# First block's gates and branch products with the tokens on the partitions, and their sum turned for the mixing projection

## The chip, the cores and the metric

The kernel runs on one core of a Trainium2 chip. The metric is the device time of one execution in microseconds (us). TensorE is called PE below, its weight load PEld, VectorE DVE, ScalarE ACT, GpSimd POOL and SyncE SP.

## The reference

Two transformer blocks, one after the other, on 256 tokens of width 1024, in fp32. The change touches the end of the first block's mixer:

```python
h = rms_norm(x, mix_norm_g[l])
(c_b, c_c, c_u, f_q, f_k, f_v, f_g, s_q, s_k, s_v, gate_logits) = split_proj(h @ w_in[l])
y_conv = short_conv_branch(c_b, c_c, c_u, conv_w[l])
y_fox = fox_branch(f_q, f_k, f_v, f_g, forget_bias[l])
y_swa = swa_sink_branch(s_q, s_k, s_v, rel_bias, sink[l])
gates = jax.nn.sigmoid(gate_logits.reshape(b, s, N_BRANCH, D_MODEL))
merged = (gates[:, :, 0] * (y_conv @ w_branch[l, 0])
          + gates[:, :, 1] * (y_fox @ w_branch[l, 1])
          + gates[:, :, 2] * (y_swa @ w_branch[l, 2]))
x = x + merged @ w_mix_out[l]
x = x + cross_attention(rms_norm(x, xattn_norm_g[l]), ...)
```

The gate logits are a 1024 x 3072 projection, each branch product is 512 x 1024, and the mixing projection is 1024 x 1024. After this come cross attention, a SwiGLU feed-forward, and the whole second block (a bidirectional recurrent mixer, spatial gating, another feed-forward).

## The kernel before, in words

**Units.** All weights are read once, in units of 128 rows x 2048 fp32 values (1 MB), 4 contraction tiles of 128 by 512 output columns for most matrices. A unit passes three stages, each with three buffers: SP fetches it (`raw`), ACT copies it rounded to fp32r (`whi`, function `hi`, L1102), and DVE takes the difference (`wlo`, function `lo`, L1672). PE then multiplies three times: high by high, high by low, low by high. The activations are split the same way (`HA`, `Y`, `MG`, each a high and a low tile). A `hi` waits for the load and for PE to be done with the unit three before it, a `lo` waits for its `hi`, a fetch waits for the `lo` three units back. Each engine's program is written out by hand in `sync`, `tensor`, `scalar` and `vector`, and runs in that order: a waiting instruction holds all that stand behind it.

**Two ways to multiply a unit.** `unit` (matmul on L523) puts channels on the partitions: the weight tile of 128 x 128 is loaded into the array and the 256 tokens stream through, so a unit is 16 tile pairs by 3 products = 48 matmuls of 256 columns. `unit_tm` (L578) puts tokens on the partitions: the activation tile is loaded and 512 weight columns stream, so a unit is 2 token halves x 4 tiles x 3 = 24 matmuls of 512 columns. Before the change `unit_tm` serves the value projections only. `turn` (L587) transposes a token-major tile with 8 PE transposes of 128 x 128.

**The stage.** After the attention projections PE runs, in this order: 12 units of gate logits (`gate0` to `gate5`, two units each), with one step of the two windowed attentions after each unit (`attention`: values, transposes of the probabilities, scores); then the branch products `br00`, `br01`, `br02` (left half of the output columns, one unit each), two `turn`s that bring the residual input (`x2`) into channel-major form, `br10`, `br11`, `br12` (right half), and the mixing projection `mo0`, `mo1`, whose four units alternate: `mo0` first half of the contraction, `mo1` first half, `mo0` second half, `mo1` second half. The first two need only the left half of the merged sum (`("mg", 0)`), the last two the right half (`("mg", 1)`).

DVE evacuates each gate (times the row of inverse roots, L1712), ACT applies tanh in place (L1248). DVE multiplies gate and branch product (L1899) and adds (L1903) into `mg`; ACT rounds half of it to `mg_hi` (L1253); DVE takes the rest as `mg_lo` (L1696). On ACT the `hi` of the units `mo0` second half and the three after it (`hi_for_pair(hi, "mo")`) stand right behind the `mg_hi` of the right half. PSUM is four banks `ps0` to `ps3` of 1024 columns each.

Of the kernel before, what the change touches and what calls it, by code (L numbers as in the profile page):

```python
# [95 lines left out]
def build(nc, d, out):  # L96
    def at(name, shape, dt, kb):
        return nc.alloc_sbuf_tensor_at(name, shape, dt, offset=BASE + int(kb * KB))
# [32 lines left out]
    xV = at("xv", [P, 2, 1024], F32, 128)  # L131
    mk = at("mk", [P, 7, P], F32, 160)
    g_tm = at("g_tm", [P, P], F32, 170)
    gates = at("gates", [P, 24, T], F32, 160)
    fq = at("fq", [P, 4, T], F32, 184)
    fk = at("fk", [P, 4, T], F32, 188)
    fv = at("fv", [P, 2, 512], F32, 192)
# [12 lines left out]
    PT = [at(f"pt{i}", [P, 384], F32, 140.5 + 1.5 * i) for i in range(2)]  # L150
    small = at("small", [32, 896], F32, 120)
    bt = at("bt", [8, 384], F32, 124)
    mg = [at(f"mg{i}", [P, 4, T], F32, 184 + 4 * i) for i in range(2)]
    mt = at("mt", [P, 4, T], F32, 192)
    MG = (at("mg_hi", [P, 8, T], F32R, 128), at("mg_lo", [P, 8, T], F32R, 136))
    x_tm2 = at("x_tm2", [P, 2, 1024], F32, 196)
    nsq = at("nsq", [P, 8, T], F32, 164)
# [72 lines left out]

    def wide(ap):
        return ap.rearrange("p (m t) -> p m t", t=T)

    def rows4(R, nm=4):
        return R[:, :].unsqueeze(1).broadcast_to([P, nm, T])
# [259 lines left out]
    def tensor(e):  # L495
# [59 lines left out]
        def linear(name, H, s, ready=None, free=None, between=None, K=8, **kw):  # L555
            for i in range(len(U[name])):
                unit(name, i, H, s, ready, free if i == 0 else None, K, **kw)
                if between is not None:
                    between(i)
# [5 lines left out]
                    if between is not None:  # L565
                        between(2 * i + g)

        def unit_tm(name, i, H, s, free=None, ncol=512):
            n, k0, nk = U[name][i]
            wh, wl = weights(n)  # L570
            if free is not None:
                e.wait_ge(*free)
            arrived(n)
            for t in range(2):
                for kk in range(nk):
                    k = k0 + kk
                    for j, (a, b) in enumerate(((wh, H[0]), (wh, H[1]), (wl, H[0]))):
                        mm = e.matmul(banks[s][:, t * 512:t * 512 + ncol], b[:, k, t * P:(t + 1) * P], a[:, kk, 0:ncol],  # L578
                                      start=k == 0 and j == 0, stop=k == 7 and j == 2, skip_group_check=True)
            mm.then_inc(*unit_done.up(("unit", n)))  # L580

        def turn(name, src, s, g, free):
            if free is not None:
                e.wait_ge(*free)
            for k in range(4):
                for t_ in range(2):
                    mm = e.transpose(banks[s][:, k * T + t_ * P:k * T + t_ * P + P],  # L587
                                     src[:, t_, (4 * g + k) * P:(4 * g + k + 1) * P], ident[:, :])
                if k % 2:
                    mm.then_inc(*pe_turn.up((name, g, k // 2)))  # L590
# [211 lines left out]
        linear("cu", HA, 0, None, v_evac.on("sk"), lambda i: attention(4 + i))  # L802
        linear("cb", HA, 1, None, v_evac.on("cc"), lambda i: attention(6 + i))
        for g in range(6):
            free = v_evac.on(("cu", "cb")[g]) if g < 2 else v_evac.on(f"gate{g - 2}")
            linear(f"gate{g}", HA, g % 2, None, free, lambda i: attention(8 + 2 * g + i))

        def y_ready(i):  # L810
            def of(k):
                if i == 0:
                    return v_split.on("conv")
                return v_split.on(("y", 2 * k + 1 + (0 if i == 1 else 8)))
            return of

        Y = (YH, YL)
        linear("br00", Y, 0, y_ready(0), v_evac.on("gate4"), K=4)
        linear("br01", Y, 1, y_ready(1), v_evac.on("gate5"), K=4, off=4)
        linear("br02", Y, 2, y_ready(2), v_soft.on(("max", 15)), K=4, off=8)  # L820
        e.wait_ge(s_x2, 16)
        turn("x2", x_tm2, 3, 0, a_soft.on(("pt", 15)))
        turn("x2", x_tm2, 0, 1, v_evac.on("br00"))
        linear("br10", Y, 1, None, v_evac.on("br01"), K=4)
        linear("br11", Y, 2, None, v_evac.on("br02"), K=4, off=4)
        linear("br12", Y, 3, None, a_evac.on(("x2", 0)), K=4, off=8)
        both(("mo0", "mo1"), MG, (0, 1), lambda k: v_split.on(("mg", k // 4)),
             (a_evac.on(("x2", 1)), v_evac.on("br10")))

# [39 lines left out]
        def ox_ready(k):  # L869
            return v_split.on(("ox", k // 2))  # L870

        linear("mk0", MN, 2, None, v_evac.on("br11"))
        linear("mk1", MN, 3, None, v_evac.on("br12"))
        unit("xq0", 0, HA, 1, h_ready("mo"), v_evac.on(("mo", 3)))
        column_sums("xattn", nsq, 2, v_evac.on("mk0"), 2, lambda k: v_stat.on(("fold", "xattn")))
        unit("xq0", 1, HA, 1, h_ready("mo"))
# [215 lines left out]
    def scalar(e):  # L1092
# [148 lines left out]
        for i in range(6):  # L1241
            for u, _, _ in U[f"gate{i}"]:
                hi(u + 2)
                attention(t)
                t += 1
            gi = gates[:, 4 * i:4 * i + 4, :]
            e.wait_ge(*v_evac.on(f"gate{i}"))
            e.activation(gi, gi, ACT.Tanh, bias=zero, scale=0.5).then_inc(*a_stat.up(("gate", i)))  # L1248

        for g in range(2):  # L1250
            hi_for(f"br{g}0", f"br{g}1", f"br{g}2")
            e.wait_ge(*v_stat.on(("merged", g)))
            e.activation(MG[0][:, 4 * g:4 * g + 4, :], mg[g][:, :, :], ACT.Copy, scale=0.5).then_inc(*a_split.up(("mg", g)))  # L1253
            if g == 0:
                for j in range(2):
                    e.wait_ge(*pe_turn.on(("x2", j, 1)))
                    e.activation(X[:, 4 * j:4 * j + 4, :], banks[(3, 0)[j]][:, :], ACT.Copy).then_inc(*a_evac.up(("x2", j)))

        def add_into(name, gain):
            for g in range(4):  # L1260
# [405 lines left out]
    def vector(e):  # L1666
        def lo(n):
            if n >= len(units):
                return
            r, h, l = slots(n)  # L1670
            e.wait_ge(*hi_done.on(n))
            e.tensor_tensor(l, r, h.bitcast(F32), ALU.subtract).then_inc(*lo_done.up(n))  # L1672

        def lo_for(*names):
            for name in names:
                for u, _, _ in U[name]:
                    lo(u + 2)
# [205 lines left out]
        for i in range(6):  # L1883
            for k, (u, _, _) in enumerate(U[f"gate{i}"]):
                lo(u + 2)
                attention(8 + 2 * i + k)
            evac(f"gate{i}", i % 2, gates[:, 4 * i:4 * i + 4, :], Rw)

        for g in range(2):
            for i in range(3):
                lo_for(f"br{g}{i}")
                name, s = f"br{g}{i}", ((0, 1, 2), (1, 2, 3))[g][i]
                gt = gates[:, 8 * i + 4 * g:8 * i + 4 * g + 4, :]
                e.wait_ge(*a_stat.on(("gate", 2 * i + g)))
                e.wait_ge(*whole(name))
                dst = mg[g] if i == 0 else mt
                e.scalar_tensor_tensor(out=dst[:, :, :], in0=gt, scalar=1.0, in1=wide(banks[s][:, :]), op0=ALU.add,  # L1899
                                       op1=ALU.mult).then_inc(*v_evac.up(name))  # L1900
                if i:
                    e.wait_ge(*v_evac.on(name))
                    e.tensor_tensor(mg[g][:, :, :], mg[g][:, :, :], mt[:, :, :],  # L1903
                                    ALU.add).then_inc(*v_stat.up(("merged", g) if i == 2 else ("merging", g)))
                    if i == 1:
                        e.wait_ge(*v_stat.on(("merging", g)))
            split_lo(("mg", g), MG[0][:, 4 * g:4 * g + 4, :], MG[1][:, 4 * g:4 * g + 4, :], mg[g][:, :, :], 0.5)

        def add_half(name, linear, s, i, gain, bias_ready=None):
            for j in range(2):  # L1910
# [520 lines left out]
```

## Time and profile before

| | us |
|---|---|
| median of 3 runs | 1113.0 |
| lowest, highest | 1109.52, 1115.24 |
| profiled execution, its own time | 1111.22 |
| its span in the trace | 1109.4 |
| PE, PEld busy | 1085.9, 993.5 |
| DVE, ACT busy | 753.5, 602.4 |
| mean granted PE clock | 0.994 |

The span is the time between the first and last instruction in the trace; 1.8 us of the execution lie outside it. All starts below are in us from the span's start. A row of the timeline gives start, duration, engine, line, operation, output<-inputs, shapes and how many instructions are merged in it; in brackets stands the idle time of the engine before them and what ended it. A matmul's duration there includes the time in which the next one already streams, so what one costs in a row of many is the distance between starts.

### The profile page before, as it was taken

The numbers are of one execution on the slowest core, as the hardware profiler recorded it, in microseconds if no ns is written. First come the engines' busy times: TensorE is split into PE (matmuls) and PEld (weight loads), VectorE is DVE, ScalarE is ACT, GpSimd is POOL, SyncE is SP. The second block draws the span as 40 slices with busy tenths as digits, with TensorE's granted clock in tenths as the row PEclk, the third lists the DMA queues.
The fourth block names the chain that finished last, engine by engine and source line by source line (L and its number), as shares of the span: only waits on it lengthen the run. The fifth ranks groups of instructions, "written<-read, shape, count | busy, mean of one in ns | idle before, by whom it ended". The sixth has DMA issues, their size and how long they took to land.

```text
span 1109.4 us, 17301 instructions
## 1 busy us (share of the span) xinstructions
PE 1085.9 (98%) x7412; PEld 993.5 (90%) x7412; DVE 753.5 (68%) x873; ACT 602.4 (54%) x720; POOL 52.9 (5%) x32
## 2 busy tenths in 40 slices
PE   8999999999999999999999999999999899999997
PEld 7998888999998988888889899999999788888886
DVE  5465765567745378776558896689938787776463
ACT  5533355543535365445446985598654575555343
POOL 0000000000000000000000260006200000000000
PEclk9999999999999999999999999999999999999998
DMA  9953243465453457565665455443434546665631
GB/s 309 220 165 120 102 136 131 140 202 191 158 205 130 129 162 249 168 189 167 195 191 176 133 155 180 122 153 124 155 140 142 190 152 198 186 196 159 229 114 38
DMA packets 140459, 183.14 MB, mean 165 GB/s; under 512 B 14036, under 2 KB 91072, under 8 KB 140384
## 3 DMA queue, kind: packets, MB, share of 16 engines
q1 hardware_dynamic: 140120, 181.73, 51.5%
q8 instruction: 58, 0.95, 0.3%
q10 hardware_dynamic: 264, 0.32, 0.1%
q14 instruction: 17, 0.14, 0.0%
HBM read 180.79 MB, written 1.25 MB: 164 GB/s over the span
## 4 chain that ended last, share of the span: by engine, by line
PE 86%; DVE 6%; ACT 5%; issue 2%; DMA 1%; SPq 0%; DVEq 0%; ACTq 0%
PE ps L523 36%; PE ps L547 21%; PE ps L549 11%; PE ps L578 5%; PE ps L950 3%; DVE wlo L1672 2%; ACT whi L1102 1%; PE ps L623 1%; DMA raw<-in_w_in 1%; PE ps L768 1%; PE ps L743 1%; ACT ha L1627 1%; PE ps L755 1%; DVE ha L2329 1%; PE ps L865 1%
## 5 line engine op out<-in xcount | busy, mean ns | idle before, releaser
L1672 DVE TENSOR_TENSOR wlo<-raw,whi 128x2048 fp32r<-128x2048 f32 (+2 forms) x170 | 379.3, 2234 | 185.2 <-ACT whi L1102 185.0
L1102 ACT ACTIVATE whi<-raw 128x2048 fp32r<-128x2048 f32 (+2 forms) x170 | 315.2, 1858 | 84.5 <-PE ps L523 39.7
L523 PE MATMUL ps<-ha,whi 128*128 128x256 f32 (+1 forms) x1856 | 342.1, 286 | 4.1 <-DVE ha L2329 2.6
L523 PEld LDWEIGHTS ps<-ha,whi 128*128 128x128 f32 (+1 forms) x1856 | 289.7, 192 | 12.2 <-issue 8.4
L523 PE MATMUL ps<-ha,wlo 128*128 128x256 f32 (+1 forms) x928 | 263.2, 284 | 0.0
L547 PE MATMUL ps<-ha,whi 128*128 128x512 f32 x640 | 224.5, 395 | 0.4 <-DVE wlo L1672 0.4
L549 PE MATMUL ps<-ha,wlo 128*128 128x256 f32 x640 | 179.5, 280 | 0.0
L523 PEld LDWEIGHTS ps<-ha,wlo 128*128 128x128 f32 (+1 forms) x928 | 178.0, 192 | 0.2
L547 PEld LDWEIGHTS ps<-ha,whi 128*128 128x128 f32 x640 | 120.0, 187 | 28.8 <-issue 0.8
L547 PE MATMUL ps<-pr,whi 128*128 128x512 f32 x352 | 123.3, 395 | 0.0
L549 PEld LDWEIGHTS ps<-ha,wlo 128*128 128x128 f32 x640 | 120.9, 189 | 0.0
L549 PE MATMUL ps<-pr,wlo 128*128 128x256 f32 x352 | 98.7, 280 | 0.0
L547 PEld LDWEIGHTS ps<-pr,whi 128*128 128x128 f32 x352 | 66.0, 187 | 15.5
L2369 POOL TENSOR_TENSOR xf<-xf,pf 128x512 f32<-128x512 f32 x14 | 31.7, 2267 | 744.0 <-DVE pb L2078 700.1
L549 PEld LDWEIGHTS ps<-pr,wlo 128*128 128x128 f32 x352 | 66.5, 189 | 0.0
L1344 ACT ACTIVATE silu<-silu 128x512 f32<-128x512 f32 x22 | 13.9, 632 | 61.9 <-DVE silu L2004 61.9
L578 PE MATMUL ps<-whi,ha 128*128 128x512 f32 x128 | 40.0, 394 | 0.6 <-DVE wlo L1672 0.6
L1339 ACT ACTIVATE silu<-ps 128x512 f32<-128x512 f32 x22 | 13.1, 597 | 44.2 <-PE ps L549 40.2
L950 PE MATMUL ps<-qt,kt 128*128 128x128 f32 x256 | 32.3, 281 | 1.9 <-DVE am L2115 1.9
L950 PEld LDWEIGHTS ps<-qt,kt 128*128 128x128 f32 x256 | 31.2, 197 | 2.4 <-issue 2.0
L2101 DVE TENSOR_TENSOR qt<-qt,q 128x1024 f32<-128x1024 f32 x16 | 28.1, 1759 | 3.4 <-ACT qt L1387 3.1
L578 PEld LDWEIGHTS ps<-whi,ha 128*128 128x128 f32 x128 | 23.5, 188 | 5.6 <-DVE wlo L1672 1.0
(372 smaller groups left out, 1713.2 us busy)
## 6 DMA issues: line engine op xcount, KB each, us to landing
raw<-in_w_in SPq DMA_DIRECT2D x55, 1024.0 KB, 5.3
raw<-in_w_ffn_gate SPq DMA_DIRECT2D x11, 1024.0 KB, 5.1
raw<-in_w_ffn_up SPq DMA_DIRECT2D x11, 1024.0 KB, 5.1
raw<-in_w_gate SPq DMA_DIRECT2D x11, 1024.0 KB, 5.1
raw<-in_w_up SPq DMA_DIRECT2D x11, 1024.0 KB, 5.1
raw<-in_w_xkv SPq DMA_DIRECT2D x8, 1024.0 KB, 5.0
raw<-in_w_ffn_down SPq DMA_DIRECT2D x8, 1024.0 KB, 4.9
raw<-in_w_down SPq DMA_DIRECT2D x8, 1024.0 KB, 4.9
```

What stands on the lines that cost most here:

```text
L523: mm = e.matmul(ps[0:width, m * T:(m + 1) * T], a[:, kk, m * width:(m + 1) * width], b[:, off + k, :], start=k == 0 and j == 0 and m % 2 = ...
L547: e.matmul(banks[s][:, at_:at_ + 512], wh[:, kk, c], H[2][:, :, k, :], start=k == 0, stop=False, skip_group_check=True)
L549: mm = e.matmul(banks[s][:, at_ + T:at_ + 512], wl[:, kk, c], H[0][:, k, :], start=False, stop=k == K - 1, skip_group_check=True)
L578: mm = e.matmul(banks[s][:, t * 512:t * 512 + ncol], b[:, k, t * P:(t + 1) * P], a[:, kk, 0:ncol], start=k == 0 and j == 0, stop=k == 7 an ...
L623: e.matmul(banks[ss[i]][:, at_:at_ + 512], wh[:, k, c], H[2][:, :, k, :], start=k == 0, stop=False, skip_group_check=True)
L950: mm = e.matmul(Sb[w][:, m * P:(m + 1) * P], Kt[b][:, m, w * P:(w + 1) * P], Q_[:, m, wq_ * P:(wq_ + 1) * P], start=m == 0, stop=True, ski ...
L1102: e.activation(h, r, ACT.Copy).then_inc(*hi_done.up(n))
L1339: e.activation(silu[w][:, :, :], split_sums(ss[2 * (i % 2)])[1], ACT.Copy).then_inc(*a_evac.up(f"{b}g{i}"))
L1344: e.activation(silu[w][:, :, :], silu[w][:, :, :], ACT.Silu).then_inc(*a_stat.up((f"silu {b}", i)))
L1672: e.tensor_tensor(l, r, h.bitcast(F32), ALU.subtract).then_inc(*lo_done.up(n))
L2101: e.tensor_tensor(Qt[b][:, :, :], Qt[b][:, :, :], q[:, :, :], ALU.mult).then_inc(*v_mix.up(("qt", i, n)))
L2369: e.tensor_tensor(Xfl, Xfl, Pfu[:, :, h - 1:h].broadcast_to(shp), ALU.add).then_inc(*p_mix.up(("xf", i, n)))
```

## The change

Gates 0 to 5 and the six branch products are made by `unit_tm` instead of `unit`. The gate's tile is laid out as 6 x 2 token halves x 512 channels. Since a token is now a partition, its inverse root is a per-partition scale: ACT reads the logits from PSUM and applies tanh with half that root (`half r`, one small DVE instruction early on) as scale, in two instructions of 512 columns for each gate, and DVE's evacuation of the gates is gone. DVE forms the merged sum token-major in one tile `mg`. Each half of the sum is then turned by PE (8 transposes) into a PSUM bank, from which ACT makes `mg_hi` and DVE `mg_lo`. The banks of the branch products are dealt anew.

```diff
-        def unit_tm(name, i, H, s, free=None, ncol=512):
+        def unit_tm(name, i, H, s, free=None, ncol=512, K=8, off=0):
...
         for g in range(6):
-            free = v_evac.on(("cu", "cb")[g]) if g < 2 else v_evac.on(f"gate{g - 2}")
-            linear(f"gate{g}", HA, g % 2, None, free, lambda i: attention(8 + 2 * g + i))
+            free = v_evac.on(("cu", "cb")[g]) if g < 2 else a_stat.on(("gate", g - 2))
+            for i in range(2):
+                unit_tm(f"gate{g}", i, HA, g % 2, free if i == 0 else None)
+                attention(8 + 2 * g + i)
...
-        linear("br00", Y, 0, y_ready(0), v_evac.on("gate4"), K=4)
-        linear("br01", Y, 1, y_ready(1), v_evac.on("gate5"), K=4, off=4)
-        linear("br02", Y, 2, y_ready(2), v_soft.on(("max", 15)), K=4, off=8)
+        e.wait_ge(*v_split.on("conv"))
+        unit_tm("br00", 0, Y, 2, v_soft.on(("max", 15)), K=4)
+        e.wait_ge(*v_split.on(("y", 7)))
+        unit_tm("br01", 0, Y, 0, a_stat.on(("gate", 4)), K=4, off=4)
+        e.wait_ge(*v_split.on(("y", 15)))
+        unit_tm("br02", 0, Y, 1, a_stat.on(("gate", 5)), K=4, off=8)
         e.wait_ge(s_x2, 16)
         turn("x2", x_tm2, 3, 0, a_soft.on(("pt", 15)))
-        turn("x2", x_tm2, 0, 1, v_evac.on("br00"))
-        linear("br10", Y, 1, None, v_evac.on("br01"), K=4)
-        linear("br11", Y, 2, None, v_evac.on("br02"), K=4, off=4)
-        linear("br12", Y, 3, None, a_evac.on(("x2", 0)), K=4, off=8)
+        turn("x2", x_tm2, 2, 1, v_evac.on("br00"))
+        unit_tm("br10", 0, Y, 0, v_evac.on("br01"), K=4)
+        e.wait_ge(*v_stat.on(("merged", 0)))
+        turn("mg", mg, 1, 0, v_evac.on("br02"))
+        unit_tm("br11", 0, Y, 3, a_evac.on(("x2", 0)), K=4, off=4)
+        unit_tm("br12", 0, Y, 2, a_evac.on(("x2", 1)), K=4, off=8)
+
+        def turn_merged(at_):
+            if at_ == 1:
+                e.wait_ge(*v_stat.on(("merged", 1)))
+                turn("mg", mg, 3, 1, v_evac.on("br11"))
+
         both(("mo0", "mo1"), MG, (0, 1), lambda k: v_split.on(("mg", k // 4)),
-             (a_evac.on(("x2", 1)), v_evac.on("br10")))
+             (v_evac.on("br10"), v_split.on(("mg", 0))), turn_merged)
...
-            gi = gates[:, 4 * i:4 * i + 4, :]
-            e.wait_ge(*v_evac.on(f"gate{i}"))
-            e.activation(gi, gi, ACT.Tanh, bias=zero, scale=0.5).then_inc(*a_stat.up(("gate", i)))
+            e.wait_ge(*whole(f"gate{i}"))
+            e.wait_ge(*v_stat.on("half r"))
+            for t_ in range(2):
+                mm = e.activation(gates[:, i, t_, :], tokens(i % 2)[:, t_, :], ACT.Tanh, bias=zero,
+                                  scale=sc[:, 24 + t_:25 + t_])
+            mm.then_inc(*a_stat.up(("gate", i)))
 
         for g in range(2):
-            hi_for(f"br{g}0", f"br{g}1", f"br{g}2")
-            e.wait_ge(*v_stat.on(("merged", g)))
-            e.activation(MG[0][:, 4 * g:4 * g + 4, :], mg[g][:, :, :], ACT.Copy, scale=0.5).then_inc(*a_split.up(("mg", g)))
+            hi_for(*(("br00", "br01", "br02", "br10") if g == 0 else ("br11", "br12")))
...
+            e.wait_ge(*pe_turn.on(("mg", g, 1)))
+            e.activation(MG[0][:, 4 * g:4 * g + 4, :], wide(banks[(1, 3)[g]][:, :]), ACT.Copy, scale=0.5).then_inc(
+                *a_split.up(("mg", g)))
...
         diagonal("x", 22)
+        e.tensor_scalar(sc[:, 24:26], sc[:, 22:24], 0.5, None, ALU.mult).then_inc(*v_stat.up("half r"))
...
             for k, (u, _, _) in enumerate(U[f"gate{i}"]):
                 lo(u + 2)
                 attention(8 + 2 * i + k)
-            evac(f"gate{i}", i % 2, gates[:, 4 * i:4 * i + 4, :], Rw)
...
             for i in range(3):
-                lo_for(f"br{g}{i}")
+                if (g, i) != (1, 0):
+                    lo_for(f"br{g}{i}")
...
-            split_lo(("mg", g), MG[0][:, 4 * g:4 * g + 4, :], MG[1][:, 4 * g:4 * g + 4, :], mg[g][:, :, :], 0.5)
+            if g == 0:
+                lo_for("br10")
+            split_lo(("mg", g), MG[0][:, 4 * g:4 * g + 4, :], MG[1][:, 4 * g:4 * g + 4, :], wide(banks[(1, 3)[g]][:, :]), 0.5)
```

The order moves at two places. In both, lines after the change are some 7 to 20 higher: L529 is L523, L584 is L578, L594 is L587, L1115 is L1102, L1271 is L1257, L1273 is L1253.

PE, at the end of `mo1` first half (bank `ps1`) and the start of `mo0` second half (`ps0`, weights in buffer 2); before:

```order
L523 MATMUL ps1<-mg_hi_104,whi1_53 128x256
L523 MATMUL ps1<-mg_lo_105,whi1_53 128x256
L523 MATMUL ps1<-mg_hi_104,wlo1_56 128x256
L523 MATMUL ps0<-mg_hi_104,whi2_54 128x256 [waits dve_split,dve_lo]
L523 MATMUL ps0<-mg_lo_105,whi2_54 128x256
```

and after:

```order
L529 MATMUL ps1<-mg_lo_104,whi1_53 128x256
L529 MATMUL ps1<-mg_hi_103,wlo1_56 128x256
L594 MATMUL ps3<-ident_60,mg_101 128x128 [waits dve_evac,dve_stat]
L594 MATMUL ps3<-ident_60,mg_101 128x128 x7
L529 MATMUL ps0<-mg_hi_103,whi2_54 128x256 [waits dve_split,dve_lo]
L529 MATMUL ps0<-mg_lo_104,whi2_54 128x256
```

The turn of the right half of the sum now stands directly ahead of the first unit that reads what is made from it.

ACT, from the third branch product's weights to the mixing projection's; before:

```order
L1102 ACTIVATE whi1_53<-raw1_50 128x2048 [waits pe_unit,ld_raw1]
L1253 ACTIVATE mg_hi_104<-mg0_101 128x1024 [waits dve_stat]
L1257 ACTIVATE xres_67<-ps3 128x1024 [waits pe_turn]
L1257 ACTIVATE xres_67<-ps0 128x1024 [waits pe_turn]
L1102 ACTIVATE whi2_54<-raw2_51 128x2048 [waits pe_unit,ld_raw2]
L1102 ACTIVATE whi0_52<-raw0_49 128x2048 [waits pe_unit,ld_raw0]
L1102 ACTIVATE whi1_53<-raw1_50 128x2048 [waits pe_unit,ld_raw1]
L1253 ACTIVATE mg_hi_104<-mg1_102 128x1024 [waits dve_stat]
L1102 ACTIVATE whi2_54<-raw2_51 128x2048 [waits pe_unit,ld_raw2]
```

and after:

```order
L1115 ACTIVATE whi2_54<-raw2_51 128x2048 [waits pe_unit,ld_raw2]
L1271 ACTIVATE xres_67<-ps3 128x1024 [waits pe_turn]
L1271 ACTIVATE xres_67<-ps2 128x1024 [waits pe_turn]
L1273 ACTIVATE mg_hi_103<-ps1 128x1024 [waits pe_turn]
L1115 ACTIVATE whi0_52<-raw0_49 128x2048 [waits pe_unit,ld_raw0]
L1115 ACTIVATE whi1_53<-raw1_50 128x2048 [waits pe_unit,ld_raw1]
L1273 ACTIVATE mg_hi_103<-ps3 128x1024 [waits pe_turn]
L1115 ACTIVATE whi2_54<-raw2_51 128x2048 [waits pe_unit,ld_raw2]
```

In both orders the `hi` of `mo0` second half (`whi2`, the last row) stands behind the second `mg_hi`; that one waited for DVE's sum and now waits for PE's turn.

## Rows read from the trace of the kernel before

**Rows 1.** The page: engines' busy time and share of span, and the chain.

```profile
span 1109.4 us, 17301 instructions
...
PE 1085.9 (98%) x7412; PEld 993.5 (90%) x7412; DVE 753.5 (68%) x873; ACT 602.4 (54%) x720; POOL 52.9 (5%) x32
...
PE 86%; DVE 6%; ACT 5%; issue 2%; DMA 1%; SPq 0%; DVEq 0%; ACTq 0%
```

**Rows 2.** The chain that ended last, from 224 us: start, us, what.

```profile
224.46 17.46 PE ps L523 x144
241.92 1.75 PE ps L587 x16
```

**Rows 3.** PE's timeline, one `unit` between two blocks of L950.

```profile
639.82 0.48 PE L523 MATMUL ps<-ha,whi 128*128 128x256 f32 x2
...
640.26 0.40 PE L523 MATMUL ps<-ha,whi 128*128 128x256 f32 x2
...
640.62 0.40 PE L523 MATMUL ps<-ha,whi 128*128 128x256 f32 x2
...
645.66 1.95 PE L950 MATMUL ps<-qt,kt 128*128 128x128 f32 x16
```

**Rows 4.** PE's timeline, one `unit_tm` between two blocks of L950.

```profile
661.88 0.71 PE L578 MATMUL ps<-whi,ha 128*128 128x512 f32 x2
...
662.65 0.62 PE L578 MATMUL ps<-whi,ha 128*128 128x512 f32 x2
...
663.33 0.62 PE L578 MATMUL ps<-whi,ha 128*128 128x512 f32 x2
...
667.41 1.95 PE L950 MATMUL ps<-qt,kt 128*128 128x128 f32 x16
```

**Rows 5.** The gates' tile: line, engine, count, ns min/median/max, first and last start.

```profile
L1712 DVE TENSOR_TENSOR gates<-ps,rw x6: 1215/1218/1220, 150.5 to 225.3; 128x1024 f32<-128x1024 f32 x6
L1248 ACT ACTIVATE gates<-gates,sc x6: 1149/1150/1153, 151.7 to 226.5; 128x1024 f32<-128x1024 f32 x6
```

**Rows 6.** The page's groups: busy us, mean ns of one, idle before.

```profile
L1339 ACT ACTIVATE silu<-ps 128x512 f32<-128x512 f32 x22 | 13.1, 597 | 44.2 <-PE ps L549 40.2
```

**Rows 7.** ACT's timeline, from the first turn to `mo`.

```profile
245.50 1.92 ACT L1257 ACTIVATE xres<-ps 128x1024 f32<-128x1024 f32 x2
...
263.56 1.06 ACT L1253 ACTIVATE mg_hi<-mg 128x1024 fp32r<-128x1024 f32 x1 [6.37 <-DVE mg L1903]
264.52 1.90 ACT L1102 ACTIVATE whi<-raw 128x2048 fp32r<-128x2048 f32 x1
...
272.55 1.92 ACT L1102 ACTIVATE whi<-raw 128x2048 fp32r<-128x2048 f32 x1 [3.84 <-PE ps L523]
```

**Rows 8.** DVE's timeline, the same stretch.

```profile
264.65 1.23 DVE L1696 SCALAR_TENSOR_TENSOR mg_lo<-mg,mg_hi 128x1024 fp32r<-128x1024 f32 x1 [1.13 <-ACT mg_hi L1253]
266.45 4.59 DVE L1672 TENSOR_TENSOR wlo<-raw,whi 128x2048 fp32r<-128x2048 f32 x2 [0.57 <-ACT whi L1102]
```

**Rows 9.** PE's longest wait: for what, us in total, times, longest.

```profile
PE ps L1079 <- DVE xres L2347: 2.9, 1, 2.9
```

**Rows 10.** Stretches: from:to, length, PE busy (instructions), granted clock, DMA share, GB/s.

```profile
76.00:77.00 1.00, 1.00 (x7) 0.50 0.00 0
...
766.00:768.00 2.00, 0.13 (x2) 1.00 0.00 0
768.00:770.00 2.00, 2.00 (x13) 0.66 0.75 190
770.00:772.00 2.00, 2.00 (x11) 0.50 0.91 332
...
874.00:878.00 4.00, 2.13 (x14) 1.00 1.06 365
```

**Rows 11.** PE's timeline where the clock was low, and one wait.

```profile
76.89 0.63 PE L523 MATMUL ps<-ha,whi 128*128 128x256 f32 x2
...
77.53 0.63 PE L523 MATMUL ps<-ha,whi 128*128 128x256 f32 x2
...
767.88 3.07 PE L950 MATMUL ps<-qt,kt 128*128 128x128 f32 x16 [1.87 <-DVE am L2115]
```

More of the change, by code:

```diff
@@ L133, in build @@
     g_tm = at("g_tm", [P, P], F32, 170)
-    gates = at("gates", [P, 24, T], F32, 160)
+    gates = at("gates", [P, 6, 2, 512], F32, 160)
     fq = at("fq", [P, 4, T], F32, 184)
@@ L152, in build @@
     bt = at("bt", [8, 384], F32, 124)
-    mg = [at(f"mg{i}", [P, 4, T], F32, 184 + 4 * i) for i in range(2)]
-    mt = at("mt", [P, 4, T], F32, 192)
+    mg = at("mg", [P, 2, 1024], F32, 184)
+    mt = at("mt", [P, 2, 512], F32, 192)
     MG = (at("mg_hi", [P, 8, T], F32R, 128), at("mg_lo", [P, 8, T], F32R, 136))
@@ L232, in wide, with tokens, merged @@
         return ap.rearrange("p (m t) -> p m t", t=T)
+    def tokens(s):
+        return banks[s][:, :].rearrange("p (t n) -> p t n", t=2)
+    def merged(g):
+        return mg[:, :, 512 * g:512 * g + 512]
     def rows4(R, nm=4):
@@ L577, in unit_tm @@
                     for j, (a, b) in enumerate(((wh, H[0]), (wh, H[1]), (wl, H[0]))):
-                        mm = e.matmul(banks[s][:, t * 512:t * 512 + ncol], b[:, k, t * P:(t + 1) * P], a[:, kk, 0:ncol],
-                                      start=k == 0 and j == 0, stop=k == 7 and j == 2, skip_group_check=True)
+                        mm = e.matmul(banks[s][:, t * 512:t * 512 + ncol], b[:, off + k, t * P:(t + 1) * P],
+                                      a[:, kk, 0:ncol], start=k == 0 and j == 0, stop=k == K - 1 and j == 2,
+                                      skip_group_check=True)
             mm.then_inc(*unit_done.up(("unit", n)))
@@ L804, in tensor @@
         for g in range(6):
-            free = v_evac.on(("cu", "cb")[g]) if g < 2 else v_evac.on(f"gate{g - 2}")
-            linear(f"gate{g}", HA, g % 2, None, free, lambda i: attention(8 + 2 * g + i))
[L810 to L815, printed above, removed]
-        Y = (YH, YL)
-        linear("br00", Y, 0, y_ready(0), v_evac.on("gate4"), K=4)
-        linear("br01", Y, 1, y_ready(1), v_evac.on("gate5"), K=4, off=4)
-        linear("br02", Y, 2, y_ready(2), v_soft.on(("max", 15)), K=4, off=8)
+            free = v_evac.on(("cu", "cb")[g]) if g < 2 else a_stat.on(("gate", g - 2))
+            for i in range(2):
+                unit_tm(f"gate{g}", i, HA, g % 2, free if i == 0 else None)
+                attention(8 + 2 * g + i)
+        Y = (YH, YL)
+        e.wait_ge(*v_split.on("conv"))
[4 more added lines that the diff above has]
+        unit_tm("br02", 0, Y, 1, a_stat.on(("gate", 5)), K=4, off=8)
         e.wait_ge(s_x2, 16)
         turn("x2", x_tm2, 3, 0, a_soft.on(("pt", 15)))
-        turn("x2", x_tm2, 0, 1, v_evac.on("br00"))
-        linear("br10", Y, 1, None, v_evac.on("br01"), K=4)
-        linear("br11", Y, 2, None, v_evac.on("br02"), K=4, off=4)
-        linear("br12", Y, 3, None, a_evac.on(("x2", 0)), K=4, off=8)
+        turn("x2", x_tm2, 2, 1, v_evac.on("br00"))
[8 more added lines that the diff above has]
+                turn("mg", mg, 3, 1, v_evac.on("br11"))
         both(("mo0", "mo1"), MG, (0, 1), lambda k: v_split.on(("mg", k // 4)),
-             (a_evac.on(("x2", 1)), v_evac.on("br10")))
+             (v_evac.on("br10"), v_split.on(("mg", 0))), turn_merged)
         def h_ready(name):
@@ L870, in ox_ready @@
             return v_split.on(("ox", k // 2))
-        linear("mk0", MN, 2, None, v_evac.on("br11"))
-        linear("mk1", MN, 3, None, v_evac.on("br12"))
+        linear("mk0", MN, 2, None, v_evac.on("br12"))
+        linear("mk1", MN, 3, None, v_split.on(("mg", 1)))
         unit("xq0", 0, HA, 1, h_ready("mo"), v_evac.on(("mo", 3)))
@@ L1256, in scalar @@
                     e.wait_ge(*pe_turn.on(("x2", j, 1)))
-                    e.activation(X[:, 4 * j:4 * j + 4, :], banks[(3, 0)[j]][:, :], ACT.Copy).then_inc(*a_evac.up(("x2", j)))
+                    e.activation(X[:, 4 * j:4 * j + 4, :], banks[(3, 2)[j]][:, :], ACT.Copy).then_inc(*a_evac.up(("x2", j)))
+            e.wait_ge(*pe_turn.on(("mg", g, 1)))
+            e.activation(MG[0][:, 4 * g:4 * g + 4, :], wide(banks[(1, 3)[g]][:, :]), ACT.Copy, scale=0.5).then_inc(
+                *a_split.up(("mg", g)))
         def add_into(name, gain):
@@ L1886, in vector @@
                 attention(8 + 2 * i + k)
-            evac(f"gate{i}", i % 2, gates[:, 4 * i:4 * i + 4, :], Rw)
         for g in range(2):
             for i in range(3):
-                lo_for(f"br{g}{i}")
-                name, s = f"br{g}{i}", ((0, 1, 2), (1, 2, 3))[g][i]
-                gt = gates[:, 8 * i + 4 * g:8 * i + 4 * g + 4, :]
+                if (g, i) != (1, 0):
+                    lo_for(f"br{g}{i}")
+                name, s = f"br{g}{i}", ((2, 0, 1), (0, 3, 2))[g][i]
                 e.wait_ge(*a_stat.on(("gate", 2 * i + g)))
                 e.wait_ge(*whole(name))
-                dst = mg[g] if i == 0 else mt
-                e.scalar_tensor_tensor(out=dst[:, :, :], in0=gt, scalar=1.0, in1=wide(banks[s][:, :]), op0=ALU.add,
+                dst = merged(g) if i == 0 else mt[:, :, :]
+                e.scalar_tensor_tensor(out=dst, in0=gates[:, 2 * i + g], scalar=1.0, in1=tokens(s), op0=ALU.add,
                                        op1=ALU.mult).then_inc(*v_evac.up(name))
@@ L1902, in vector @@
                     e.wait_ge(*v_evac.on(name))
-                    e.tensor_tensor(mg[g][:, :, :], mg[g][:, :, :], mt[:, :, :],
+                    e.tensor_tensor(merged(g), merged(g), mt[:, :, :],
                                     ALU.add).then_inc(*v_stat.up(("merged", g) if i == 2 else ("merging", g)))
```

## The prediction, made before the run

> **What bounds the kernel now.** I read the page first: PE is busy in 98% of the span and carries 86% of the chain that ended last; DVE is at 68%, ACT at 54% [rows 1]. PE's longest single wait in the whole span is 2.9 us, at its very end [rows 9]. So PE's own instruction stream sets the time, and other engines count only where they make PE wait. In the stage that is changed the chain is PE alone: 144 matmuls, 16 transposes, matmuls again [rows 2]. A cheaper stream on PE is therefore a gain in full, and a new wait on PE a loss in full; changes on DVE and ACT are worth nothing by themselves.
>
> **The matmuls.** What a matmul costs is the distance between starts. With channels on the partitions three matmuls of 256 columns take 640.62 - 640.26 = 0.36 us [rows 3], so a unit of 48 is 16 x 0.36 = 5.76 us; the chain has 144 of them, three units, in 17.46 us, 5.82 each [rows 2]. With tokens on the partitions three matmuls of 512 columns take 663.33 - 662.65 = 0.68 us [rows 4], and a unit of 24 is 8 x 0.68 = 5.44 us. The columns that stream are the same, 12288; what differs is the number of matmuls. 0.12 us for 256 columns and 0.227 for 512 fit columns at 2.4 GHz plus 13 ns for each matmul, and 24 fewer of these are the 0.32 us. Between blocks of other work, as the gates stand between attention steps, the whole unit with its start takes 645.66 - 639.82 = 5.84 us in one form and 667.41 - 661.88 = 5.53 us in the other [rows 3, 4]: 0.31 us. I take 0.31 for all 18 units (12 of gates, 6 of branches): **-5.6 us**, ends 5.2 and 5.8 (0.29 and 0.32 each).
>
> Here a rule speaks against the change. The Trainium skill, page "TensorE: Matmul & The Clock Gate", section "Back-to-back issue gap", gives N/2.4 + 2.5 ns for one matmul of N columns at full clock. By that a unit would go from 48 x 109.2 ns to 24 x 215.8 ns, from 5.24 to 5.18 us, and all 18 would save 1.1 us, not 5.6. The rows show 120 and 227 ns, so the trace does not agree, and I follow the rows.
>
> **The two turns of the sum** add 16 PE transposes of 128 x 128. The same two turns of the residual input take 1.75 us in the chain [rows 2]: **+1.75 us**, all on the path, since PE has nothing else then. The first turn waits for the left half of the sum. DVE has it some 2.5 us after the third branch product (two instructions of 1.2), and PE has two turns and a whole unit in between, 7.2 us: no wait. The branch products take new banks; each waits for an evacuation at least one unit old.
>
> **DVE and ACT.** DVE loses six evacuations of 1.22 us [rows 5]. ACT's tanh goes from one instruction of 1.15 us to two of some 0.6 (reading PSUM in that form took 597 ns [rows 6]), and starts when PE ends instead of after DVE. No PE wait depended on either, so this is nothing. `mg_hi` and `mg_lo` now read PSUM; ACT's copies of 1024 columns from there took 1.92 / 2 = 0.96 us [rows 7], as from SBUF. The one DVE instruction on 2 columns early on costs 0 to 0.2 us; I take 0, it stands ahead of a `lo` that waits for ACT anyway.
>
> **The new wait.** The second turn is the place where the change costs. It stands directly ahead of `mo0` second half, which reads what is made from it. And on ACT the `hi` of that very unit's weights stands behind the second `mg_hi`. Before, that `mg_hi` waited for DVE's sum and ran at 263.56, the `hi` at 264.52, and the `lo` was done at 266.45 + 2.29 = 268.7; PE came to the unit at about 272.5, where it frees the next buffer [rows 7, 8]. It was 3.8 us early. Now `mg_hi` cannot start before PE has finished `mo1` first half and the turn. From there everything is in series: `mg_hi` until ACT takes the next instruction, 264.52 - 263.56 = 0.96; `hi` 1.90; `lo` 4.59 / 2 = 2.29 [rows 7, 8]; and three handovers of 0.03 to 0.05 (266.45 after 264.52 + 1.90 is 0.03). That is 5.25 us of idle PE, and 0.2 us more that a turn needs to drain, in which PE would otherwise have gone on. `mg_lo`, 1.23 us on DVE, fits beside the `hi`. **+5.4 us**, ends 5.2 and 6.0. Nothing hides it: the only work that could, three more units, is queued behind it on PE. What is queued behind on ACT and DVE is the weights of the next three units. The second of them is ready 2.2 us after the first, PE needs it 5.8 us after; the fetches held back by the late `lo` have three units' time against 5 us of load. So there is no second wait.
>
> **The clock after it.** No wait of that length is in the trace, so its effect on the clock has to be bounded. After an idle time of 1.87 us the granted clock fell: 1.00 while idle, then 0.66 and 0.50 (1.2 GHz) in two stretches of 2 us [rows 10, 11]: by shares 2 x 0.34 / 0.5 = 1.4 and 2.0, together 3.4 us at the lower level. In another place, idle for nearly as long (2.13 busy of 4 us), it stayed at 1.00; and once it was 0.50 without any idle time [rows 10]. At 1.2 GHz three matmuls take 77.53 - 76.89 = 0.64 us [rows 11] for 0.36, so 3.4 us at that level lose 3.4 x (1 - 0.36 / 0.64) = 1.5 us. The bounds are 0, and 16 x 0.28 = 4.5 us if the whole unit after the wait runs slow. 5.3 us is nearly three times the wait that was enough, so I take the nearest row: **+1.5 us**.
>
> **Sum.** -5.6 + 1.75 + 5.4 + 1.5 = +3.05 us. The profiled execution took 1111.2 us (span 1109.4 and 1.8 around it), so its like would take 1114.3 us. It lay 1.8 us under the median of the three runs, 1113.0; the mean of all four executions is 1112.2, the best guess of the level. **1115.3 us**, 0.3% more than that level and 0.2% more than the median: no change that can be told, since a measurement of this kernel can tell about 0.5%, 5.6 us.
>
> **Rivals.**
> - *The clock holds through the wait.* For it speaks the place where a wait nearly as long left it at 1.00 [rows 10]; against it that here PE idles almost three times longer. 1113.8 us, chance 0.15.
> - *Slower: the clock stays low for the whole of `mo0` second half.* Place: the 48 matmuls after the wait; price 4.5 us instead of 1.5; it decides from where the low stretch outlasts the idle time by 10 us (16 x 0.64). For it: the idle time is long. Against: in the rows the clock came back some 4 us after PE did. +6.05 us, 1118.3 us, just at the border of measurably slower. Chance 0.12.
> - *The wait does not come, or is hidden:* I misjudge what PE or ACT is held by. Then -5.6 + 1.75 = -3.85 us, 1108.3 us, 0.35% faster. A shorter form of it: only `mg_hi` and `mg_lo`, 0.96 + 1.23 = 2.3 us, stand in PE's way. Against both speaks the order on ACT, where the `hi` is plainly behind. Together 0.12.
> - *The form of the matmul saves little:* streaming alone counts. The columns are equal, so the saving would be nothing: 1.75 + 5.4 + 1.5 = +8.65 us, 1120.9 us. For it: 12288 columns a unit either way. Against it: both forms stand in this trace, 0.31 us apart [rows 3, 4]. Chance 0.03. The gap that the Trainium skill gives (page and section above) lies near this case, at 1.1 us saved and 1119.8 us.
> - Something that I do not see: 0.05.
>
> **How the numbers follow.** The forecast has the rest, 0.53. A single comparison moves by some 2 us. Slower by over 0.5% (above 1118.6): half of the slow-clock rival, all of the fourth, a little of the forecast: 0.14. Faster by over 0.5% (below 1107.4): a third of the hidden-wait rival and part of the unseen: 0.05. Within 0.5%: 0.81. The range runs from 1109.0, which leaves out half of the case without the wait, to 1120.0, which takes in the slow clock.
>
> **What would show it.** In the profile of the changed kernel: PE distances of 0.68 us for three matmuls in gates and branches, 18 units each 0.31 us shorter; stage from the first gate to the end of `br12` shorter by 5.6 less 0.9 us of the first turn; one PE wait of 5.2 to 5.3 us on DVE's `wlo` ahead of `mo0` second half, the longest of the span; on ACT `mg_hi`, then `whi`, without a gap; the granted clock at 0.5 in the stretch behind the wait; from `mk0` on nothing different. The forecast is wrong if PE waits there under 3 us, if a second wait follows in `mo` or `mk0`, or if the gates' stage turns out to wait for tanh.

## The result: 0.45% slower

Over 20 executions each, the changed kernel takes 1115.2 us (1110.67 to 1120.52) and the kernel before 1111.05 us (1105.43 to 1115.24). The ratio is 1.0045, with a 95% interval of 1.0029 to 1.0061: 5.0 us slower, a difference that is there, but just under the half per cent named in the prediction. (The means, 1115.63 and 1110.62 us, lie 5.0 us apart, as the ratio has it; the medians 4.15.) A second comparison gave 1.0043 (1.0018 to 1.0068). One of the 23 executions of the kernel before in it took 1176.7 us at a mean granted clock of 0.847 and is in no ratio. The median of 1113.0 that was shown ahead of the change came from three executions and was some 2 us high; the forecast of 1115.3 us met the time, but the added time was forecast as 3.05 us and is 5.0.

The page of the changed kernel, to be held against [rows 1]:

```profile
span 1116.2 us, 16478 instructions
...
PE 1087.9 (97%) x6996; PEld 975.1 (87%) x6996; DVE 746.0 (67%) x868; ACT 603.7 (54%) x726; POOL 55.3 (5%) x32
```

PE has 416 matmuls fewer (432 less 16 transposes) and yet is busy for 2.0 us longer. In the stage itself, from the first matmul of `gate0` to the first of `mk0` (the unit after `mo`), it is busy for 153.7 us where it was for 153.9: what the matmuls save there is taken up by the new turns and by matmuls at half clock, which count with their longer durations. Of the 2.0 us, 1.7 come ahead of the stage and 0.5 behind it, where nothing of weight was changed.

The waits of PE, longest in total first (for what, us, times, longest), against [rows 9]:

```profile
PE ps L529 <- DVE wlo L1689: 5.2, 1, 5.2
PE ps L1092 <- DVE xres L2366: 3.5, 2, 2.9
PE ps L642 <- DVE nsq L2287: 2.7, 1, 2.7
```

The first is new, and longer than anything that the kernel before has. The chain around it (start, us, what) answers to [rows 2]:

```profile
221.58 16.59 PE ps L584 x72
238.17 1.75 PE ps L594 x16
239.92 5.46 PE ps L584 x24
245.38 0.87 PE ps L594 x8
246.26 10.92 PE ps L584 x48
257.18 11.51 PE ps L529 x96
268.69 0.89 PE ps L594 x8
269.80 0.72 issue
270.52 1.91 ACT whi L1115
272.46 2.30 DVE wlo L1689
274.81 43.19 PE ps L529 x336
```

Three branch units take 16.59 us where they took 17.46. After the last turn, at 269.6, the chain leaves PE: `mg_hi` holds ACT till 270.52, then come the weights' `hi` and `lo`, and PE goes on at 274.81. ACT and DVE at that place, against [rows 7, 8]; here the `hi` is the first of three merged in a row, and ACT's rows stand ahead of DVE's:

```profile
269.60 1.02 ACT L1273 ACTIVATE mg_hi<-ps 128x1024 fp32r<-128x1024 f32 x1 [15.84 <-PE ps L594]
270.52 5.50 ACT L1115 ACTIVATE whi<-raw 128x2048 fp32r<-128x2048 f32 x3
```

```profile
270.66 1.23 DVE L1713 SCALAR_TENSOR_TENSOR mg_lo<-ps,mg_hi 128x1024 fp32r<-128x1024 f32 x1 [10.89 <-ACT mg_hi L1273]
272.46 6.70 DVE L1689 TENSOR_TENSOR wlo<-raw,whi 128x2048 fp32r<-128x2048 f32 x3 [0.57 <-ACT whi L1115]
```

ACT had been idle for 15.84 us before, with that `hi` next but one in its program and everything it needs at hand (its load, and a buffer free since the third branch product of the right half ended at 257.2; in experiment 2 it does run at that point). And the clock (from:to, length, PE busy, granted clock, DMA share, GB/s), against [rows 10]:

```profile
270.00:272.00 2.00, 0.00 (x0) 1.00 0.00 0
272.00:274.00 2.00, 0.00 (x0) 0.99 0.00 0
274.00:276.00 2.00, 1.19 (x5) 0.50 0.11 7
276.00:278.00 2.00, 2.00 (x12) 0.50 0.88 299
278.00:280.00 2.00, 2.00 (x11) 0.50 1.05 377
280.00:282.00 2.00, 2.00 (x16) 0.80 1.00 321
```

It fell at the end of the idle time and stayed at 1.2 GHz until about 281, some 6 us after PE had resumed.

**How the stage is measured below.** One execution differs from the next by up to 1%, so I read from each trace the time from the first matmul of `gate0` to the first of `mk0`, from their starts in the timeline. Each row is one trace unless it says two. In the kernel before that is 129.87 to 283.81, 153.94 us. The two units of `mo` behind the wait take 2 x 5.76 = 11.52 us at full clock, and what the stretch from their first matmul to `mk0` takes beyond that is the clock's share.

| kernel | stage, us | against before | PE idle ahead of `mo0` second half | clock's share behind it |
|---|---|---|---|---|
| before | 153.94 | | 0 | 0 |
| changed | 158.98 | +5.04 | 5.2 | 2.7 |
| changed, second trace | 158.36 | +4.42 | 5.2 | 2.1 |
| turn early (two traces) | 150.85 | -3.09 | 0 | 0 |
| turn early, weights first (two traces) | 150.85 | -3.09 | 0 | 0 |
| weights first | 155.04 | +1.10 | 2.5 | 1.55 |
| filled | 156.35 | +2.41 | 0.2 (the rest filled) | 0.1 |
| halved | 162.64 | +8.70 | 5.2 | 1.55 |
| before, held | 161.23 | +7.29 | 4.3 | 2.8 |
| before, held and filled | 158.53 | +4.59 | 0.25 (the rest filled) | 0.1 |

The ratios below are each against executions of the kernel before that were made beside the experiment (their medians are 1110.87 us for experiments 1 to 4, 1110.84 for 5, 6 and the first part of 7, 1110.42 for the last part). They are not quotients of the medians: for the kernel held that would be 1.0072 and not 1.0051.

### The profile page after: what moved, and what is told of

Read it like the earlier page. It is cut to its first block, busy times and chain, and to the rows that moved or that the text cites. A ratio compares the mean times of both kernels' runs of the same rounds, so it can differ in the third digit from the quotient of the medians.

```text
span 1116.2 us, 16478 instructions
## 1 busy us (share of the span) xinstructions
PE 1087.9 (97%) x6996; PEld 975.1 (87%) x6996; DVE 746.0 (67%) x868; ACT 603.7 (54%) x726; POOL 55.3 (5%) x32
## 4 chain that ended last, share of the span: by engine, by line
PE 86%; ACT 6%; DVE 5%; issue 2%; DMA 1%; SPq 0%; DVEq 0%; ACTq 0%
PE ps L529 27%; PE ps L553 21%; PE ps L584 14%; PE ps L555 11%; PE ps L963 3%; DVE wlo L1689 2%; ACT whi L1115 2%; PE ps L630 1%; PE ps L775 1%; PE ps L750 1%; ACT ha L1644 1%; PE ps L762 1%; DVE ha L2348 1%; PE ps L878 1%; PE ps L632 1%
## 5 line engine op out<-in xcount | busy, mean ns | idle before, releaser
L1115 ACT ACTIVATE whi<-raw 128x2048 fp32r<-128x2048 f32 (+2 forms) x170 | 315.0, 1858 | 88.6 <-PE ps L555 35.1
L529 PE MATMUL ps<-ha,whi 128*128 128x256 f32 (+1 forms) x1472 | 273.0, 287 | 2.6 <-DVE ha L2348 2.6
L529 PEld LDWEIGHTS ps<-ha,whi 128*128 128x128 f32 (+1 forms) x1472 | 231.4, 193 | 7.7 <-issue 3.8
L529 PE MATMUL ps<-ha,wlo 128*128 128x256 f32 (+1 forms) x736 | 209.8, 285 | 0.0
L529 PEld LDWEIGHTS ps<-ha,wlo 128*128 128x128 f32 (+1 forms) x736 | 142.2, 193 | 0.2
L584 PE MATMUL ps<-whi,ha 128*128 128x512 f32 x320 | 100.7, 396 | 0.6 <-DVE wlo L1689 0.6
L584 PEld LDWEIGHTS ps<-whi,ha 128*128 128x128 f32 x320 | 58.6, 188 | 15.7 <-issue 3.3
L2388 POOL TENSOR_TENSOR xf<-xf,pf 128x512 f32<-128x512 f32 x14 | 34.2, 2442 | 742.5 <-DVE pb L2097 702.2
L584 PE MATMUL ps<-wlo,ha 128*128 128x512 f32 x160 | 62.5, 390 | 0.0
L584 PEld LDWEIGHTS ps<-wlo,ha 128*128 128x128 f32 x160 | 30.0, 188 | 6.6
```

The source lines that it names most:

```text
L529: mm = e.matmul(ps[0:width, m * T:(m + 1) * T], a[:, kk, m * width:(m + 1) * width], b[:, off + k, :], start=k == 0 and j == 0 and m % 2 = ...
L584: mm = e.matmul(banks[s][:, t * 512:t * 512 + ncol], b[:, off + k, t * P:(t + 1) * P], a[:, kk, 0:ncol], start=k == 0 and j == 0, stop=k = ...
L1115: e.activation(h, r, ACT.Copy).then_inc(*hi_done.up(n))
L2388: e.tensor_tensor(Xfl, Xfl, Pfu[:, :, h - 1:h].broadcast_to(shp), ALU.add).then_inc(*p_mix.up(("xf", i, n)))
```

## The experiments

**1. The turn one unit earlier.** If the wait and its clock are the whole loss, room between the turn and its reader must remove it.

```diff
         def turn_merged(at_):
-            if at_ == 1:
+            if at_ == 0:
                 e.wait_ge(*v_stat.on(("merged", 1)))
```

> The changed kernel with the second turn of the sum one unit earlier, behind mo0 first half instead of behind mo1 first half; nothing else differs. Theory: the added time is the wait of 5.2 us ahead of mo0 second half and the low clock after it; with a whole unit (5.76 us) between the turn and its reader the series mg_hi, hi, lo (5.2 us) just fits, the wait is gone and the clock stays at 1.00. What is left is the matmuls' saving (some 4.9 us) less the two turns (1.75 us): about 3.2 us less than the kernel before, ratio 0.997, and 8 us less than the changed kernel. Rival: the changed kernel loses its time elsewhere in the stage (gates, tanh, banks); then it stays at or above the kernel before, ratio 1.000 to 1.004.

Measured: ratio 0.9991 (0.9969 to 1.0014), 1109.12 us. The chain in its trace:

```profile
256.21 5.75 PE ps L529 x48
261.96 0.87 PE ps L594 x8
262.84 46.07 PE ps L529 x384
```

The turn stands between the units and nothing follows it but matmuls; in 268 to 274 us the granted clock is 1.00. The room is narrow: the unit's `lo` ends at 268.03 and PE comes to it at 268.42. The stage is 3.09 us shorter than before the change and 8.13 shorter than the changed kernel's. So the loss was the wait and the clock behind it, and the rival is out. The total is less clear: 0.9991 is 1.0 us, not 3.1, though the interval holds both.

**2. The weights ahead of the sum's split.** The turn stays, ACT and DVE split `mo0` second half's weights before `mg_hi` and `mg_lo`.

```diff
+            if g == 1:
+                hi(U["mo0"][1][0])
             e.wait_ge(*pe_turn.on(("mg", g, 1)))
...
+            else:
+                lo(U["mo0"][1][0])
             split_lo(("mg", g), ...)
```

(The pair loops that follow leave this unit out.)

> The changed kernel with the turn left where it is, but on ACT and DVE the split of mo0 second half's weights stands ahead of mg_hi and mg_lo. Theory: 2.9 of the 5.2 us of the wait are the weights' hi and lo queued behind mg_hi (they run ahead of mg_lo's end by that much); what remains is mg_hi 0.96 plus mg_lo 1.23 and handovers, 2.3 us. The clock after 2.3 us may or may not fall (0 to 1.5 us). Against the kernel before: -4.9 + 1.75 + 2.5 + 0 to 1.5, that is -0.7 to +0.9 us, ratio 0.999 to 1.001. Rival: the order on ACT does not matter, because PE waits for the turn's result alone; then the wait stays at 5.2 us and the time at the changed kernel's.

Measured: 0.998 (0.9955 to 1.0005), 1108.72 us. That is below the expected 0.999 to 1.001, of which the interval reaches all but the top. The stage of its trace is 1.10 us longer than before the change, which would be 1.0010, just outside. By time alone this kernel cannot be told from that of experiment 1; what follows rests on the one trace. One of its waits, and the chain there:

```profile
PE ps L529 <- DVE mg_lo L1716: 2.5, 1, 2.5
```

```profile
266.62 0.89 PE ps L594 x8
267.50 0.02 issue
267.52 1.03 ACT mg_hi L1275
268.56 0.02 issue
268.58 1.24 DVE mg_lo L1716
269.82 0.14 issue
269.95 40.11 PE ps L529 x320
```

The wait is halved and now ends on `mg_lo`: the order on ACT and DVE made up 2.7 of the 5.2 us, and the sum's own split, which no order can take away behind the turn, the other 2.5. The clock fell all the same, to 0.65 in the mean of 272 to 276 us, and took 1.55 us.

**3. The wait filled.** 42 unused matmuls on PE while it waits.

```diff
                 turn("mg", mg, 3, 1, v_evac.on("br11"))
+                e.wait_ge(*v_evac.on("br12"))
+                for _ in range(42):
+                    e.matmul(banks[2][:, 0:T], MG[0][:, 0, 0:P], MG[0][:, 0, :], start=True, stop=True)
```

> The changed kernel with 42 more matmuls of 256 columns into the idle bank ps2, right behind the second turn, where PE waits; their result is not used. 42 x 0.12 = 5.0 us of the 5.2 us of idle time are filled. Theory: the low clock after the wait (0.50 from about 274 to 281 us in the changed kernel's trace) costs 2.7 us by itself and is caused by the idle time; filled, the granted clock stays at 1.00 there and the kernel is 2.7 us faster than the changed one, some 2.3 us slower than the kernel before, ratio 1.002. Rival: the clock's share of the loss is nothing or comes whatever PE does there; then the ratio stays at the changed kernel's 1.0045.

Measured: 1.0006 (0.9983 to 1.0029), 1110.8 us; the changed kernel's 1.0045 lies outside that interval. Its clock at the place:

```profile
268.00:272.00 4.00, 4.00 (x34) 1.00 0.01 4
272.00:276.00 4.00, 3.78 (x32) 1.00 0.65 208
276.00:280.00 4.00, 4.00 (x35) 1.00 1.02 348
```

PE does 5 us of work for nothing and the stage is 2.63 us shorter than the changed kernel's (156.35 against 158.98). That agrees with the 2.7 us read behind the wait, but it uses the same trace of the changed kernel; against that kernel's second trace it is 2.0 us. The idle time brought the low clock, and what the low clock costs is not one fixed figure.

**4. The matmuls halved.** 512 columns as two matmuls of 256, tokens still on the partitions.

```diff
-                        mm = e.matmul(banks[s][:, t * 512:t * 512 + ncol], b[:, off + k, ...], a[:, kk, 0:ncol], ...)
+                        for c in range(0, ncol, step):
+                            mm = e.matmul(banks[s][:, t * 512 + c:t * 512 + c + step], b[:, off + k, ...],
+                                          a[:, kk, c:c + step], ...)
```

> The changed kernel with every 512-column matmul of the gates and branch products split into two of 256 columns with the same stationary tile: 48 matmuls a unit again, tokens on the partitions as before. Theory: what the change saves is a fixed time of some 13 ns for each matmul, not anything about which side is stationary; the distance between starts goes back to 0.12 us, a unit to 5.76 us, and the kernel takes 18 x 0.3 = 5 to 5.8 us more than the changed one, ratio to the kernel before 1.009. Rival: streaming counts alone or the saving is due to the operands' roles; then it stays within 1 us of the changed kernel, ratio 1.0045 to 1.005.

Measured: 1.007 (1.0044 to 1.0095), 1119.06 us. In its chain the branch products read

```profile
224.10 17.46 PE ps L586 x144
```

the same 17.46 us for 144 matmuls as channels on the partitions took [rows 2]. So the saving is a fixed time for each matmul and has nothing to do with which side is stationary. One thing stays unseparated: each of the two halves is given a weight load of its own (PEld x7638 in this kernel, x7206 in the changed one), so the time may belong to the matmul or to the load that comes with it. The whole is 3.66 us more than the changed kernel's stage, less than the 5 expected, because here the clock behind the wait took 1.55 us and not 2.7: from `gate0` to the last turn it is 143.45 against 138.63 us, 4.8 more.

**5. The wait put into the kernel before**, with nothing else of the change.

```diff
+        e.wait_ge(*unit_done.on(("unit", U["mo1"][0][0])))
         hi_for_pair(hi, "mo")
```

> The kernel BEFORE the change, with one wait added on ACT: the hi of mo0 second half's weights may start only when PE has finished mo1 first half. Nothing else is touched. It makes the changed kernel's wait without its matmul forms and turns. Theory: hi 1.90 and lo 2.29 in series leave PE idle for 4.3 us (0.1 to 0.2 more lost), and the clock falls to half for some 6 us behind it as in the changed kernel, 2.7 us more: +7 us, ratio 1.006. Rival: the clock's loss needs the changed kernel's other work (transposes, wide matmuls); then +4.4 us, ratio 1.004, and the clock stays at 1.00 there.

Measured: 1.0051 (1.0026 to 1.0075), 1118.79 us, stage +7.29 us. The chain, and the clock behind it:

```profile
271.78 1.92 ACT whi L1102
273.70 0.02 issue
273.72 2.31 DVE wlo L1673
276.03 0.04 issue
276.07 23.96 PE ps L523 x175
```

```profile
276.00:280.00 4.00, 3.93 (x18) 0.50 0.72 214
280.00:284.00 4.00, 4.00 (x27) 0.72 1.03 350
```

One wait of 4.3 us costs 7.3: neither transposes nor wide matmuls are needed for the clock to fall.

**6. The same, filled** with 34 unused matmuls.

> The kernel held, with 34 unused matmuls of 256 columns (34 x 0.12 = 4.1 us) into the idle bank ps2 behind mo1 first half, where PE waits. Theory: the idle time is gone, the clock stays at 1.00, what is left is the series itself: +4.4 us over the kernel before, ratio 1.004, 2.7 us less than held. Rival: the two are equal, so that the clock costs nothing.

Measured: 1.0029 (1.001 to 1.0048), 1114.64 us, stage +4.59 us. 2.70 us less than held, as expected.

**7. Both repairs, and repetitions.** The early turn and the weights' order together, and the early turn once more:

> The changed kernel with both repairs: the second turn behind mo0 first half, and mo0 second half's weights split ahead of mg_hi and mg_lo. Theory: with the turn early the wait is already gone and the weights' order adds only slack, so this equals the kernel with the early turn alone: no wait ahead of mo0 second half, clock 1.00 there, stage about 3.2 us shorter than before the change, ratio 0.997. Rival: the early turn's margin (5.2 us of series against 5.6 us of cover) is sometimes missed, which the wider slack would mend; then this is faster than the early turn by 0.5 us or more.

> The same kernel as turn_early, timed once more beside early_weights, since its first interval (0.9969 to 1.0014) holds both no change and the expected 0.997. Theory: 0.997 (3.2 us less than the kernel before). Rival: the saving on PE's stream does not reach the total; 1.000.

Measured: both repairs 0.9971 (0.9948 to 0.9995), 1109.32 us; the early turn 0.9994 (0.9974 to 1.0013), 1109.83 us. The stage is 150.85 us in both traces. Two kernels with the same stage and the same program after it should not differ, so both repairs were timed again, with the changed kernel beside them:

> The same kernel as early_weights, once more. In the traces its stage is as long as that of the early turn alone (150.85 us both, 3.09 less than before the change), yet the intervals differ (0.9971 against 0.9991 and 0.9994). Theory: the two are equal and their difference is the spread of executions, in which the clock falls or does not fall at places after the stage; then this comes out between 0.996 and 0.9995. Rival: the weights' order is worth something that a trace does not show; then it stays at 0.997 or below and clear of the early turn's.

> The changed kernel itself, on the same chip as early_weights_again, for the same stage in a second execution. Theory: wait 5.2 us again; its clock loss behind the wait lies between 1.5 and 2.7 us, as it is set by when the low stretch begins and not by the kernel; stage 3.9 to 5.1 us longer than before the change. Rival: the loss belongs to the kernel and is 2.7 us again.

Measured: both repairs 0.9981 (0.9959 to 1.0002), 1108.46 us, stage 150.85; the changed kernel 1.0043, 1115.15 us, wait 5.2 us, clock's share 2.1 us (its first 4 us behind the wait were at 0.50, the next 4 at 0.86). The clock's share is thus not fixed, as the theory said.

The four comparisons of repaired kernels lie at 0.9991, 0.9994, 0.9971 and 0.9981. All four lie under 1, and their mean, 0.9984, is 1.8 us; the stage says 3.1. One interval alone excludes 1, and one alone (0.9974 to 1.0013) just misses the 0.9972 that 3.1 us would be. That a repaired kernel is faster than the kernel before is likely, by 1 to 3 us; whether the missing microsecond is real or spread is left open. The traces give a lead. From `mk0` to the end the four of the repaired kernels take 827.6 to 832.1 us, 830.0 in the mean, and the other eight 823.4 to 830.2, 826.3 in the mean; in all four the clock falls near 872 and again between 1080 and 1085 us, in the one trace of the kernel before at neither place. Whether an earlier end of the stage brings these falls about was not tested. That a repaired kernel is faster than the changed one, by some 0.6%, is beyond doubt (1.0002 and 1.0018 are the near ends of the two intervals measured side by side).

## Why the prediction was right, and where its sum was off

- **What bounds the kernel:** right. DVE's six evacuations are gone (753.5 to 746.0 us busy), the tanh moved, and PE is busy without a gap from `gate0` to the end of the branches (126.96 of 126.96 us). One price was wrong without effect: the two tanh instructions of a gate take 0.77 us each, not some 0.6 (768 ns in the median of 12), and nothing waits for them.
- **The matmuls, -5.6 us:** the mechanism is right (experiment 4), the size 0.7 too large. A branch unit takes 16.59 / 3 = 5.53 us instead of 5.82, 0.29 less. For a gate unit I took 0.31 from a place among L950 blocks. Among attention steps one unit with its step took 8.06 us (start to start in the chain, 155.34 to 163.40) and takes 7.80 (154.77 to 162.57), 0.26 less; the first triples after an attention step start 0.70 us apart, not 0.68. 12 x 0.26 + 6 x 0.29 = 4.9 us.
- **The turns, +1.75 us:** 0.87 and 0.89 us in the chain. With 4.9 that leaves 3.1 us of gain, which is the 3.09 us of the early turn's stage.
- **The rule that spoke against it:** the Trainium skill, page "TensorE: Matmul & The Clock Gate", section "Back-to-back issue gap", gives N/2.4 + 2.5 ns for a matmul by itself; the estimate from it was 1.1 us for all 18 units. Measured are 4.9 us; the trace does not agree with it.
- **The new wait, +5.4 us:** right in place, cause and size: 5.2 us of idle time, in the series `mg_hi`, `hi`, `lo`, with the drain of the turn 5.4.
- **The clock after it, +1.5 us:** the term that was mis-sized. It was 2.7 us in the trace shown and 2.1 in the second, against 1.5 taken from the loss behind a wait of 1.87 us. The bounds, 0 and 4.5, held it. That the wait was longer does not explain it: behind the same 5.2 us the halved kernel lost 1.55 us, as much as was forecast, and so did weights first behind 2.5 us.
- **The sum:** -4.9 + 1.75 + 5.4 + 2.7 = +4.95 us, close to both the stage's +5.04 and the ratio's 5.0. Forecast was +3.05. That the forecast time, 1115.3 us, came out to 0.1 us was luck: the level of the kernel before, taken as 1112.2 from four executions, is 1111.05 by twenty, so 1.15 us too high, and the added time, 4.15 us by the medians, was taken 1.1 too small. The prediction called it a change that cannot be told; in size it lies within the 0.5% meant there, but twenty executions of each do tell it.
- **The rivals:** the wait came, so the hidden wait is out. The matmul's form saved 4.9 us, so the rival by which streaming alone counts is out. The clock neither held nor stayed low for the whole unit (4.5 us); at 2.7 us it went 40% of the way from the forecast to that rival.

## What to carry to other kernels

When a result has to pass through another engine and back, count what stands between the step and its reader on every engine's program, not on the critical one alone: a ready piece of work behind a blocked one doubled this wait. Put the step at least its whole series ahead of the reader (here 5.2 us, one unit), and price a new wait of PE at its length plus the clock behind it, here 1.5 to 2.8 us more for waits of 2.5 to 5.2 us. A gain on the order of 5 us in a stream is easily paid back by one such wait; move first, then look for the one wait that the move made.

## What the runs showed of the hardware

The clock's fall is a matter of chance as well as of length. The instructions after `mk0` are the same in all these kernels, and yet in the twelve traces that part took between 823.4 us (held) and 832.1 us (both repairs, second time). The trace of the early turn has, among others, these stretches below full clock after the stage, the last two at a place where the kernel before stayed at 1.00 [rows 10]:

```profile
760.00:765.00 5.00, 3.10 (x23) 0.91 0.20 43
765.00:770.00 5.00, 5.00 (x34) 0.75 0.52 175
870.00:875.00 5.00, 2.10 (x9) 0.83 0.88 297
875.00:880.00 5.00, 4.35 (x26) 0.82 0.32 115
```

In the traces looked at the clock falls at four such places (near 76, 765, 877 and 1090 us), each in some executions and not in others: near 765 and 877 us behind waits of 1.9 to 3.1 us, near 1090 us behind two of 0.7 us, near 76 us behind none. A fall costs 1.5 to 2.8 us where it could be read, which is of the size of most changes tried here, and it is the likely source of the 1% by which executions of one kernel differ. The executions of the kernel before that were made beside the experiments agree: of the 87 (the one of 1176.7 us aside), six with a mean granted clock of 0.999 took 1106.2 us in the mean, and twelve with 0.991 took 1113.3. That is a correlation and no test. And 2.5 us of idle time were enough for a fall (experiment 2), so halving the wait did not keep the clock up.

What a fall costs does not follow the length of the wait: 1.55 us behind 2.5 us (weights first) and behind 5.2 (halved), 2.1 and 2.7 behind 5.2 in two traces of one kernel, 2.8 behind 4.3 (held). It follows how long the clock is low while PE works. In the second trace of the changed kernel it fell at 270.3 us, while PE was still idle, and 4.6 us of the low stretch lay behind PE's start at 272.5; in weights first it fell at 271.4, 1.4 us after PE had started again, and was back at 2.4 GHz by 275.
